# Hybrid decoder trunk on one core: row products of the last tokens moved from the second expert table to the routing heads

## What is computed

```python
q = (xt @ w_pq).reshape(PEER_BLOCK, PEER_HEADS, 2, PEER_HALF)
s = jnp.einsum('thpd,hpkd->thpk', q, sub_keys)
v1, i1 = lax.top_k(s[:, :, 0], PEER_TOPK)
v2, i2 = lax.top_k(s[:, :, 1], PEER_TOPK)
cand = (v1[..., :, None] + v2[..., None, :]).reshape(PEER_BLOCK, PEER_HEADS, -1)
top, pos = lax.top_k(cand, PEER_TOPK)
eidx = jnp.take_along_axis(cidx, pos, axis=-1)
g = jax.nn.softmax(top.astype(jnp.float32), axis=-1).astype(xt.dtype)
ue = u_tab[eidx]
a = jax.nn.gelu(jnp.einsum('thkd,td->thk', ue, xt))
ve = v_tab[eidx]
return jnp.einsum('thk,thkd->td', g * a, ve)
```

## Time and profile before

| | us |
|---|---|
| median of 3 runs | 3480.99 (3477.33 to 3486.32) |
| profiled execution | 3480.61, its span 3478.9 |
| TensorE (PE) busy | 3417.0 of the span |
| VectorE (DVE) busy | 2418.1 |
| ScalarE (ACT) busy | 1404.1 |
| GpSimd (POOL) busy | 1384.1 |

### The profile page before, as it was taken

The page is one execution under the profiler, slowest core; times in us unless marked ns, Lnnn a source line. Parts: engine busy times, 40 slices in busy tenths (PEclk is TensorE's granted clock), DMA queues, the critical chain, the costliest instruction groups (busy, mean ns, idle before and its releaser), DMA issues.

```text
span 3478.9 us, 53302 instructions
## 1 busy us (share of the span) xinstructions
PE 3417.0 (98%) x17974; PEld 2926.1 (84%) x17974; DVE 2418.1 (70%) x4725; ACT 1404.1 (40%) x2298; POOL 1384.1 (40%) x1291
## 2 busy tenths in 40 slices
PE   7999999999999999999999999999999999999999
PEld 5777799999999887777777777999999998777777
DVE  6455679999887775555454566799998869555554
ACT  3334343343577333333333343444346753333332
POOL 1011108676753434444401110277677325344442
PEclk9999999999999999999999999999999999999999
DMA  6375337777899989999734744577778999899995
GB/s 236 122 259 188 139 132 221 221 205 212 256 350 314 392 323 347 364 360 364 302 129 164 241 144 138 186 226 193 217 216 263 372 337 376 305 368 360 367 359 193
DMA packets 306404, 910.04 MB, mean 262 GB/s; under 512 B 69077, under 2 KB 101893, under 8 KB 305317
## 3 DMA queue, kind: packets, MB, share of 16 engines
q0 software_dynamic: 163792, 473.58, 38.9%
q1 hardware_dynamic: 105552, 383.83, 31.7%
q10 hardware_dynamic: 36868, 50.35, 3.9%
HBM read 792.14 MB, written 115.47 MB: 261 GB/s over the span
## 4 chain that ended last, share of the span: by engine, by line
PE 90%; DVE 3%; DMA 2%; POOL 2%; issue 2%; ACT 1%; ACTq 0%; SPq 0%; DVEq 0%; POOLq 0%
PE ps L463 15%; PE ps L464 15%; PE ps L465 15%; PE ps L1080 10%; PE ps L1081 9%; PE ps L1082 9%; PE ps L1094 3%; PE ps L1060 3%; PE ps L883 2%; PE ps L980 1%; PE ps L939 1%; PE ps L981 1%; PE ps L982 1%; PE ps L1020 1%; DVE urow L1727 1%
## 5 line engine op out<-in xcount | busy, mean ns | idle before, releaser
L463 PE MATMUL ps<-mov,whl 128*128 128x384 f32 (+1 forms) x2816 | 1004.9, 357 | 1.2 <-DVE whl L450 1.2
L465 PE MATMUL ps<-mov,whl 128*128 128x384 f32 (+1 forms) x2816 | 984.7, 350 | 0.0
L464 PE MATMUL ps<-mov,whl 128*128 128x384 f32 (+1 forms) x2816 | 984.5, 350 | 0.0
L450 DVE TENSOR_TENSOR whl<-raw,whl 128x1024 fp32r<-128x1024 f32 x648 | 793.0, 1224 | 226.3 <-ACT whl L440 221.6
L440 ACT CAST whl<-raw 128x1024 fp32r<-128x1024 f32 x648 | 681.2, 1052 | 101.1 <-ACT hst L1275 96.4
L1080 PE MATMUL ps<-whl,wgthl 128*128 128x512 f32 x1536 | 601.9, 392 | 4.0 <-DVE wgthl L1819 4.0
L1081 PE MATMUL ps<-whl,wgthl 128*128 128x512 f32 x1536 | 598.0, 389 | 0.0
L1082 PE MATMUL ps<-whl,wgthl 128*128 128x512 f32 x1536 | 597.5, 389 | 0.0
L463 PEld LDWEIGHTS ps<-mov,whl 128*128 128x128 f32 x2816 | 529.2, 188 | 38.8 <-issue 8.7
L465 PEld LDWEIGHTS ps<-mov,whl 128*128 128x128 f32 x2816 | 528.6, 188 | 31.7
L464 PEld LDWEIGHTS ps<-mov,whl 128*128 128x128 f32 x2816 | 529.4, 188 | 29.9 <-issue 2.2
(11 more groups left out here) (271 smaller groups left out, 3655.8 us busy)
## 6 DMA issues: line engine op xcount, KB each, us to landing
raw<-in_uT_tab SPq DMA_DIRECT2D x256, 512.0 KB, 4.3
raw<-in_v_tab SPq DMA_DIRECT2D x256, 512.0 KB, 6.7
expert_spill<-hst ACTq DMA_DIRECT2D x256, 192.0 KB
hin<-expert_spill POOLq DMA_DIRECT2D x256, 192.0 KB, 6.9
gt<-weight_spill POOLq DMA_DIRECT2D x64, 768.0 KB, 8.4
raw<-in_w_in SPq DMA_DIRECT2D x72, 512.0 KB, 11.3
raw<-in_w_mod SPq DMA_DIRECT2D x64, 512.0 KB, 3.6
weight_spill<-stage POOLq DMA_DIRECT2D x14, 2048.0 KB, 12.9
```

The lines of the kernel that those rows point to most:

```text
L450: nc.vector.tensor_tensor(whl[:, m % RING, 1], raw[:, raw_n(m) % RAW], whl[:, m % RING, 0].bitcast(F32), ALU.subtract).then_inc(lo_done, 1)
L463: nc.tensor.matmul(o, w[:, 0, k], src[:, 0, k, :cols], start=(k == 0), stop=False)
L464: nc.tensor.matmul(o, w[:, 0, k], src[:, 1, k, :cols], start=False, stop=False)
L465: mm = nc.tensor.matmul(o, w[:, 1, k], src[:, 0, k, :cols], start=False, stop=(k == KC - 1))
```

## The change

The table of products beside a head gets two more at panel 8, so that heads 1 to 7 have eight products instead of six (56 instead of 42). The remaining list shrinks: the second table has 16 products beside its first 12 panels instead of 30 beside its first 23. What GpSimd does at panel `DOTS_V` moves with it from panel 23 to panel 12. The 56 products beside the 48 panels between stay as they are. The number of buffers (`UR` = 6) stays.

```diff
 LATE_U = 2 * REST + N_G
-DOTS_H = (0, 0, 0, 0, 0, 0, 0, 0, 0, 2, 2, 2)
+DOTS_H = (0, 0, 0, 0, 0, 0, 0, 0, 2, 2, 2, 2)
 DOTS_A = sum(DOTS_H) * (PH - 1)
-DOTS_V = 23
+DOTS_V = 12
 DOTS = ([0, 0] + [2] * (REST - 2) + [1, 1, 1, 2] * (N_G // 4) + [1] * 4 + [0] * (REST - 4)
-        + [1, 1, 2] * 7 + [1, 1])
+        + [1, 1, 2] * 4)
 assert len(DOTS_H) == 2 + T_U
```

## The result

| | before | after |
|---|---|---|
| median | 3480.51 us (3477.33 to 3486.32, 4 runs) | 3516.74 us (3512.69 to 3522.99, 4 runs) |
| profiled execution, span | 3480.61, 3478.9 | 3515.35, 3513.6 |

The ratio is 1.0104 (95% interval 1.0083 to 1.0124): the change makes the kernel 36 us slower. The forecast was 3533, its range 3494 to 3548.

What follows compares the result with a forecast made beforehand. TensorE, busy 98% of the span, was taken as the bound, so only its waits count. Profiled 3480.6 us plus 52.7 of lateness (24.9 and 27.8 a layer), with second table and clock at 0, gave 3533 us; range 3494 to 3548.

Steps and rivals of the forecast that it cites:

- rival A: Routing stage: only the first head stalls, later gathers land within 6.06 us; 3495 to 3498 us, 3502 as variant; chance 0.24.
- VectorE alone has the room for eight products: In a head of 54.33 us: two more products take 2.29 us and fit in VectorE's 2.65 us of idle time.
- The seventh and eighth row come behind 16 scatters, and a loop closes: Heads: last product, indices, scatters, second gather, landing, last product take 56.97 or 57.4 us, over the 54.33 of a head.
- Head 1 is late by 9.0 and 9.4 us: First head with products: its last row lands that much after the product's start, in the first and second layer.
- The last product 1.45 us later costs at the end of head 7: End of head 7: TensorE already waits 0.6 us there for a split, so there is no room for the shift.
- The removal from the second table is worth 0: Second table: 14 products a layer fewer, gathers moved to panel 12; taken as 0, bounds -4.0 and +3 us.
- lateness at the last head: Head 7: first head's lateness plus six heads' loop growth, 24.9 us in the first layer, 27.8 in the second.
- the whole lateness shows: End of head 7: the last product's whole lateness appears in the time, together 52.7 us over both layers.
- The room of TensorE: Heads: tightest split has 1.9 us of room; with 1.9 us of idle time TensorE waits once lateness exceeds 3.8 us.
- The clock: After the first head's delay: TensorE's granted clock could fall, costing up to 1.2 us; counted as 0.
- B: Heads: products find their rows and fit; only 1.45 us at head 7's end stays in each layer; 3484 us, chance 0.05.
- C: Second table: its relief decides if head 1's delay is hidden; gain 4.0 us, 3477 us, chance 0.03.

## Why the prediction was right, and where not

**The time and the range.** The mechanism is the one that was forecast, but 52.7 us were added where 36 were measured. The 3516.7 lies under the 3522 to 3545 that the forecast's own mechanism was given; it is inside the stated range because that was drawn down to rival A, whose mechanism did not happen. That part is luck.

**What held.** *VectorE alone has the room for eight products*: shown by the kernel with eight buffers, which has them at 3485. *The seventh and eighth row come behind 16 scatters, and a loop closes*: shown by that kernel and by the one with gathers between the scatters; each opens the loop at another place, and both lose little, 2.4 and 1.4 us against the kernel before on the same chip. *Head 1 is late by 9.0 and 9.4 us*: measured 573.26 - 564.61 = 8.65, and 2307.25 - 2278.05 less the 20.45 by which the layer starts later, 8.75. *Indices 12.98, scatters to second gather 35.29*: measured 12.89 to 13.20, and 35.3 and 35.0 in the mean of heads 2 to 7. *The last product 1.45 us later costs at the end of head 7*: the wait there is 1.5 instead of 0.6 in both kernels with an open loop, 0.9 more. (By the prediction's own numbers the shift is 2.29 - 0.76 = 1.53, not 1.45, and 9.0 + 6 x 2.64 is 24.8, not 24.9; neither changes the sum by more than 0.1.) *The removal from the second table is worth 0*: its length changed by +1.4 and -1.0 us. Of the signs named, the waits for rows came (7.2 us in head 1, none in head 2, 0.3 to 1.9 in heads 3 to 6, 2.4 in head 7, in the first layer), and heads 3 to 7 were 55.3 to 56.4 us long there. TensorE's waits were 11.6 and 10.9 us a layer, of which more than half was for the searches and not for splits.

**The term that was mis-sized** is "lateness at the last head": 9.0 + 6 x 2.64 and 9.4 + 6 x 3.07. Its landing time of 8.7 and 9.1 us came from gathers of the kernel before; in the loop it is 7.1 and 7.0. (The kernel with the second table's products spread, whose routing stage is the same, has 7.2 and 7.3.) With this a head grows by 1.1 us in the first layer (12.95 + 35.34 + 7.11 - 54.33) and by 0.6 in the second (12.95 + 35.04 + 6.97), not by 2.6 and 3.1. Head 2 is another matter in both layers: its rows landed in time, some 1.6 us before they were needed, but it took 54.75 and 54.62 us, as TensorE came out of its wait late. 8.65 + 6 x 1.1 + 1.6 gives the first layer's lateness, 8.75 + 6 x 0.6 + 1.7 nearly the second's. The last product of head 7 was late by 907.40 - 890.61 = 16.8 us, and by 2638.93 - 2604.05 - 20.45 = 14.4; predicted were 24.9 and 27.8. These 16.8 and 14.4 are also just what TensorE lost in the two stages, so that the step "the whole lateness shows" held to a tenth.

I had argued that the gather keeps its place among the panel loads; that was nearly so, and it still landed sooner. The prediction put the long landing down to the panels' travelling at the same time; with loads of an eighth the kernel before shows that they are 2 us of the 8.7 in the old order of time. Two things changed together: the next panel load is issued 1.0 us after the gather before the change, and after it 0.1 us after the gather in seven of the twelve heads (in the other five 1.0 us ahead of it); and the gather's own issue, which counts in the landing time, takes 1.66 us before, and 0.97 after in those seven (1.9 to 2.0 in the others). The four traces part them roughly. In heads 2 to 6 of the first layer the two orders differ by 8.7 - 7.0 = 1.7 us with full loads and by 6.8 - 5.9 = 0.9 with loads of an eighth; of these 0.9 the longer issue is 0.7. So about half of the difference hangs on the loads, and most of the other half is the issue. Why the issue takes longer there is open, and neither was tried alone.

Of the Trainium skill's fit ("DMA: Bandwidth & Descriptors", section "Anatomy of one DMA — SWDGE (gpsimd) path"), 2.0 us plus bytes / 436e3, an estimate of 3.2 us for this gather: no run reached it. The quickest second gather in a head, with panel loads at an eighth, took 5.0, and the quickest row gather of any, in the kernel before with such loads, 4.1.

**The room of TensorE** was bound to the wrong wait. I took the split at 752.93 with 1.9 us. Behind head 1 TensorE did wait 1.3 us for a split, but 4.6 for the score matmuls, line 1020, whose bank VectorE's search must have read (`score_used`). The amount, 5.9 us, was near my 5.2.

**The clock**, which I counted at 0 with up to 1.2 us above, is 3 us in the first layer and 2 in the second when head 1 alone is late. The changed kernel has the slow matmuls too (0.71 in 590 to 600 us, 0.83 in 910 to 920). They stand in the place of waits: the loss of each stage is the lateness of its last product to a tenth, and in the heads that wait for rows that lateness is made by the loop. So my reason for the 0 holds for it, by this account and not by a run of its own; it does not hold for rival A, which I had put too low by that.

**Rival A** (only the first head stalls) was about as near to the time as the forecast: its loss in pure form, eight products in head 1 alone, gives 3499. Its condition, a landing within 6.06 us, was not met in any of heads 2 to 7. The measured 3517 lies halfway between A's 3497 and the forecast's 3533. **B** (rows found in time) is what the two repaired kernels show, at 3484 to 3485 as computed. **C** (faster by the relief) is out.

## What to carry to other kernels

An engine with idle time has room for work only if the data are there: before adding work to it, count its buffers against the uses in one round, and look what stands ahead of the refill in the issuing engine's program order. When refills wait for work of the same round, add up the loop (work, wait, issue, landing, work) and compare it with the round; a loop that is longer by 1 us costs that in every round, once the room behind it is used up. The cure here was free, two gathers moved ahead of two scatters (in head 1, of six), and of the two places tried the products were better taken from the stretch where TensorE really waited than from the one where another engine looked full.

## What the runs showed of the hardware

- A wait of TensorE of 4.6 us was followed by a stretch with a mean granted clock of 0.66 to 0.83 over 10 us, that is partly at 1.2 GHz (0.71 and, in the second layer, 0.66 in the changed kernel, where that wait was 4.5 us; 0.76 and, in the second layer, 0.83 in the one with eight products in head 1 alone). In the latter the stage lost 3 us beyond its 5.8 us of waits in the first layer and 2 beyond 5.5 in the second. The matmuls in it count as busy, so the page's 98% did not move.
- The landing time of a head's second gather (128 rows of 4 KB) was 5.0 to 10.6 us in these kernels. Cutting the traffic of panel loads to an eighth took 1.8 us off 8.7 in the kernel before (heads 2 to 6 of the first layer) and 1.1 off 7.0 in the changed one; it is no constant that can be carried from one order to another within 2 us.
